# The scan's norm: its sum over partitions behind the next application on TensorE, its reciprocal root as a power on GpSimd

## The reference, cut to what matters

```
y = y + D * x                        # scan's result, 256 tokens x 2048
y = y * silu(z)
y = y * rsqrt(mean(y*y over each group of 256 features) + 1e-5) * norm_w
mix = y @ w_out
x = layer_norm(ALPHA * x + mix, ln1_g, ln1_b)
```

## Time and profile before

| | |
|---|---|
| median of 3 runs | 2312.76 us |
| the profiled execution's own time | 2315.55 us |
| its span | 2313.7 us |
| mean granted TensorE clock | 0.996 |
| TensorE busy | 2276.5 us (98%) |
| VectorE busy | 952.4 us (41%) |
| ScalarE busy | 445.7 us (19%) |
| GpSimd busy | 74.1 us (3%) |

### The profile page before, as it was taken

The page is one execution under the profiler, slowest core; times in us unless marked ns, Lnnn a source line. Parts: engine busy times, 40 slices in busy tenths (PEclk is TensorE's granted clock), DMA queues, the critical chain, the costliest instruction groups (busy, mean ns, idle before and its releaser), DMA issues.

```text
span 2313.7 us, 25295 instructions
## 1 busy us (share of the span) xinstructions
PE 2276.5 (98%) x10678; PEld 1349.9 (58%) x10678; DVE 952.4 (41%) x1905; ACT 445.7 (19%) x1011; POOL 74.1 (3%) x130
## 2 busy tenths in 40 slices
PE   8999999999999999999999999999999999999998
PEld 6568547886487449897434333334999643333343
DVE  3567656667576556553211111123754321211122
ACT  3410003357100010220211211101032021111111
POOL 2000000000100000000000000000000000000000
PEclk9999999999999999999999999999999999999999
DMA  7279625354698414246999999995426599999997
GB/s 291 109 307 398 258 77 204 147 182 182 240 407 319 179 74 179 100 171 266 379 428 427 427 427 428 428 419 194 147 81 246 224 409 427 427 428 427 428 428 289
DMA packets 59167, 671.64 MB, mean 290 GB/s; under 512 B 7504, under 2 KB 7792, under 8 KB 18720
## 3 DMA queue, kind: packets, MB, share of 16 engines
q1 hardware_dynamic: 51888, 649.45, 69.0%
q0 software_dynamic: 7152, 20.43, 2.6%
HBM read 666.59 MB, written 3.26 MB: 290 GB/s over the span
## 4 chain that ended last, share of the span: by engine, by line
PE 88%; DMA 9%; DVE 2%; ACT 0%; issue 0%; SPq 0%; POOL 0%; DVEq 0%; POOLq 0%; ACTq 0%
PE ps L101 85%; DMA ring<-in_exp_w 6%; DMA arena<-in_exp_w 2%; PE ps L349 1%; DVE arena L114 1%; DVE arena L117 1%; PE ps L2698 1%; DMA ring<-in_ada_w 0%; PE ps L625 0%; DMA arena<-ssm_rows 0%; DMA X<-in_x 0%; PE ps L1875 0%; DVE X L117 0%; ACT arena L105 0%; PE ps L1217 0%
## 5 line engine op out<-in xcount | busy, mean ns | idle before, releaser
L101 PE MATMUL ps<-arena 128*64 128x512 f32 (+7 forms) x3956 | 937.5, 467 | 15.2 <-DMA arena<-in_exp_w 5.7
L101 PEld LDWEIGHTS ps<-arena 128*128 128x128 f32 (+2 forms) x3956 | 446.5, 166 | 462.6 <-issue 434.2
L101 PE MATMUL ps<-ring,arena 128*64 128x512 f32 (+1 forms) x1664 | 447.2, 591 | 2.6 <-DMA ring<-in_exp_w 2.6
L101 PE MATMUL ps<-XTGB,ring 128*128 128x256 f32 (+1 forms) x2160 | 423.5, 353 | 0.0
L101 PEld LDWEIGHTS ps<-XTGB,ring 128*128 128x128 f32 x2160 | 367.1, 190 | 52.8 <-issue 10.7
L101 PEld LDWEIGHTS ps<-ring,arena 128*64 128x64 f32 (+1 forms) x1664 | 163.8, 149 | 257.9 <-issue 255.0
L122 DVE COPY arena<-ps 128x512 f32<-128x512 f32 (+3 forms) x135 | 64.9, 500 | 448.5 <-PE ps L101 316.4
L121 ACT COPY arena<-ps 128x512 f32<-128x512 f32 (+3 forms) x181 | 82.7, 477 | 665.8 <-PE ps L101 293.1
L101 PE MATMUL ps<-ring,XTGB 128*128 128x512 f32 (+3 forms) x540 | 208.3, 543 | 0.1
L101 PE MATMUL ps<-XTGB,arena 128*64 128x512 f32 (+2 forms) x736 | 200.7, 428 | 0.0
L105 ACT ACTIVATE arena<-ps 128x512 f32<-128x512 f32 (+2 forms) x95 | 52.2, 555 | 722.4 <-PE ps L101 717.5
(11 more groups left out here) (150 smaller groups left out, 921.5 us busy)
## 6 DMA issues: line engine op xcount, KB each, us to landing
arena<-in_exp_w SPq DMA_DIRECT2D x90, 2048.0 KB, 26.4
ring<-in_exp_w SPq DMA_DIRECT2D x68, 2048.0 KB, 28.1
ring<-in_mlp_w SPq DMA_DIRECT2D x25, 2048.0 KB, 8.7
ring<-in_ada_w SPq DMA_DIRECT2D x20, 2048.0 KB, 9.8
XTGB<-in_exp_w SPq DMA_DIRECT2D x18, 2048.0 KB, 32.1
ring<-in_ssm_w_in SPq DMA_DIRECT2D x12, 2048.0 KB, 7.7
ring<-in_w_in SPq DMA_DIRECT2D x12, 2048.0 KB, 7.8
ring<-in_gate_w SPq DMA_DIRECT2D x12, 2048.0 KB, 7.5
```

What stands on the lines that cost most here:

```text
L101: return self.e.matmul(o, lhsT=lhsT, rhs=rhs, start=start, stop=stop, skip_group_check=True)
```

## The change

1. On TensorE `norm_b(g)` moves from the end of iteration 2g + 4 to iteration 2g + 5, behind the application there (groups 6 and 7 stay where they were). ScalarE's `norm_b` moves likewise, to behind `exps` of the odd iteration.
2. ScalarE does one Identity with scale 1/256 and bias 1e-5 instead of Ln and Exp, and announces `ymean`.
3. GpSimd raises the result to the power -0.5, over 128x256 with `half` broadcast along the row, and announces `yr`. In its program the powers stand among the row loads: power (i - 6)/2 behind load i for even i from 6, and 5 to 7 behind the last load.
4. On VectorE `norm_c` comes one pair of iterations later, for groups 6 and 7 in iterations 18 and 20.

```
+            def norm_power(g):
+                r = xcT[:, 2 * g, :]
+                pool.wait_ge(at("ymean", g), at("half"))
+                pool.then_inc(pool.tt(r, r, C["half"][:, 0:1].to_broadcast([P, T]), ALU.pow), ("yr", g))
...
             for i in range(SP):
                 if i >= 3:
                     pool.wait_ge(at("sy", i - 3))
                 pool.landed(pool.e.dma_start(s_E[i % 3][:, :, 0:512], ...
+                if i >= 6 and i % 2 == 0:
+                    norm_power((i - 6) // 2)
+            for g in range(5, 8):
+                norm_power(g)
...
  (TensorE)
                 if i in (SP, SP + 2):
                     norm_b((i - 4) // 2)
+                elif 5 <= i < SP and i % 2 == 1:
+                    norm_b((i - 5) // 2)
...
-                if 4 <= i < SP and i % 2 == 0:
-                    norm_b((i - 4) // 2)
...
  (ScalarE)
             def norm_b(g):
-                r = xcT[:, 2 * g, :]
                 act.wait_ge(at("sn", g))
-                k = act.then_inc(act.act(r, ps_of("sn", g)[:, 0:T], ACT.Ln, scale=1.0 / 256, bias=epst),
-                                 ("read", "sn", g))
-                act.wait_ge(k)
-                act.then_inc(act.act(r, r, ACT.Exp, scale=-0.5), ("yr", g))
+                act.then_inc(act.act(xcT[:, 2 * g, :], ps_of("sn", g)[:, 0:T], ACT.Identity, scale=1.0 / 256, bias=epst),
+                             ("ymean", g), ("read", "sn", g))
...
                 if i < SP:
                     exps(i)
-                if i >= 4 and i % 2 == 0 and (i - 4) // 2 < 8:
+                if i in (SP, SP + 2):
                     norm_b((i - 4) // 2)
+                elif 5 <= i < SP and i % 2 == 1:
+                    norm_b((i - 5) // 2)
...
  (VectorE)
-                if i >= 5 and i % 2 == 1 and (i - 5) // 2 < 8:
-                    norm_c((i - 5) // 2)
+                if 7 <= i < SP + 2 and i % 2 == 1:
+                    norm_c((i - 7) // 2)
+                if i in (SP + 2, SP + 4):
+                    norm_c((i - 6) // 2)
```

## The result

The changed kernel takes 2605.34 us (median of 4 runs, 2600.05 to 2607.17) against 2313.47 us before (median of 4); the ratio is 1.1251, interval 1.1238 to 1.1264. It is slower by 292 us, where 293 were predicted.

The account below looks back on a forecast made before the run. TensorE was taken to bound the scan, busy 123.33 of 125 us. Eight powers and five gaps on GpSimd delay part (3,0) by 291 us; with 2 us of restart, 2312.8 + 293 = 2606 us, range 2568 to 2642.

Parts of the forecast that it names:

- power 0 starts: GpSimd starts the first power at 513.0 us, after ScalarE's exps(5), Identity of 0.47 us and a handover of 0.1.
- one power: Each of eight 128x256 GpSimd powers takes 41.6 us, from narrower powers' cost of 0.161 us per further element.
- gap, five times: Before powers 1 to 5, GpSimd waits 8.0 us for row load, least, exps, Identity and handovers.
- power 7 ends: GpSimd's last power ends at 886.0 us: 513.0 + 8 x 41.6 + 5 x 8.0 + 0.2.
- delay of (3,0): TensorE's third of the last seven output parts starts at 887.1 instead of 596.15 us, 291 us later.
- restart of TensorE: After idling before part (3,0), TensorE loses 2 us (0 to 5), taken from the program's first eight transposes.
- The removed table loads: On ScalarE, 16 fewer table loads free 20.5 us; worth 0 to 1.7 us to the kernel, taken as 0.
- The sum behind the application: TensorE's sum moved behind the application: with cheap powers, at most 2.4 us lost; in the changed kernel, hidden.
- TensorE idle "some 290 us": TensorE idles some 290 us, nearly all ahead of applications and one output part; its busy time stays as before.
- A cheap power on a long row: On GpSimd, powers below 2.1 us hide before the row loads: no change, 2311 to 2315 us; chance 0.09.
- A price that falls with width: GpSimd's price per element falls somewhat: powers of 10 us give 2353 us, of 20 us 2433; chance 0.05.
- A gain by ScalarE's freed time: ScalarE's freed 24 us bring E earlier, limited to 1.7 us; chance 0.01 of beyond 4.6 us.

Follow-up runs that it names:

- experiment 1: Changed kernel with the eight GpSimd powers acting on only half the columns, 128 of 256; 2440.81 us.
- 5: Changed kernel with the eight GpSimd powers acting on only 32 of the 256 columns; 2323.68 us, ratio 1.0039 to the kernel before.
- 6: Changed kernel with the eight GpSimd powers acting on only 16 of the 256 columns; 2316.46 us, ratio 1.0007 to the kernel before.
- experiment 2: Changed kernel with a multiplication in the power's place on GpSimd, order, waits and queues kept; 2317.43 us, ratio 1.0011 to the kernel before.
- experiment 4: Changed kernel with all 16 row loads issued apart from the powers, on ScalarE's queue instead of GpSimd's; 2566.76 us.
- 9: Changed kernel with 78 idle multiplications of 128x512 on TensorE ahead of output part (3,0); 2604.09 us.
- 10: Changed kernel with 82 idle multiplications of 128x512 on TensorE ahead of output part (3,0); 2606.64 us.
- experiment 8: Changed order with Ln and Exp on ScalarE, moved to the even iteration ahead of the gate's copy, nothing added on GpSimd; 2315.08 us, ratio 1.0005 to the kernel before.
- experiment 3: Changed kernel's order with ScalarE's Ln and Exp instead of Identity, in the odd iteration, nothing added on GpSimd; 2321.46 us, ratio 1.0026 to the kernel before.
- experiment 7: Changed kernel with a multiplication for the power and TensorE's sum back ahead of the odd application; 2316.45 us, ratio 1.0006 to the kernel before.

## Why the prediction was right

| step | predicted | measured |
|---|---|---|
| power 0 starts | 513.0 | 512.32 |
| one power | 41.6 | 41.13 |
| gap, five times | 8.0 | 7.5 to 7.9, sum 38.7 |
| power 7 ends | 886.0 | 879.9 |
| part (3,0) starts | 887.1 | 880.93 |
| delay of (3,0) | 291 | 284.8 |
| restart of TensorE | 2 | 2.5 |

**The price of a power** carried the sum: 333 of the 373 us predicted between power 0's start and power 7's end. The step from 2 and 8 elements to 256 held within 1.1%: 159 ns per element between 8 and 128, and again between 128 and 256. Experiments 1, 5 and 6 show it, and experiment 2 shows that the loss goes with it.

**The gap** was right in its length and in its parts (chain above), and experiment 4 removed it.

**The sum** is 6 us too high in the trace: 3.8 from the powers, 1.3 from the gaps, 0.7 from the start, 0.2 from handovers. Of the 0.7, 0.6 is no error of the working: the first row load left at 474.29 in this execution, at 474.90 in the one of before. That the median still came to within 1 us of 2606 is partly luck: the profiled execution is the fastest of the four, 5.3 us under their median, and behind the scan it took 3 us less than the one of before. Where the others spent more isn't shown.

**The restart** was put at 2 us and took 2.5, but the rows that it was taken from don't bear it. The eight slow transposes of the program's start (1.95 us against 1.04) ran at a granted clock of 1.00 by the profile of before, so their slowness isn't shown to be that of an idle TensorE's clock, and why they were slow stays open. Behind the powers it was the clock, by experiments 9 and 10. This hit is luck in its size.

**The removed table loads** were put at 0. No value shows where ScalarE has slack (the stage took 115.3 us with them in experiment 8, 115.9 and 115.0 without them in 2 and 6). What I hadn't seen is that in the changed order Ln and Exp would have cost some 5 us (experiment 3 against 8); the change removes a cost there that it would itself have brought.

**The sum behind the application** was bounded, with TensorE's idle time, by -1.7 and +2.4 us for cheap powers: 0.3 to 1.2 us in single traces (experiment 7). In the changed kernel it is hidden, as said.

**Three signs were off.** TensorE idle "some 290 us" is 412 - 137 = 275 us in the scan. Of it 24 us lie ahead of the sum of group 7 (799.43), which waits for norm_c(5); the list had only applications and one output part. And its busy time was said to be as before but rose by 12.3 us: the same work at a mean clock of 0.67 takes longer. This costs nothing but at the last restart, the rest lies beside the powers. GpSimd busy 403 us (407 said), row loads 48.8 us apart (49.6), ScalarE's table loads 16 fewer, `least` waiting for loads and TensorE for VectorE: as said.

**The rivals.** A cheap power on a long row: excluded by experiment 1. A price that falls with width: excluded, the widths of 1 to 256 lie on one line. A gain by ScalarE's freed time: no run's median lies below that of before, and 1.7 us of idle TensorE time was all that could have been gained.

## What to carry to other kernels

Price an operation by its own rows at two or more widths and work out the slope; the name of the instruction form (TENSOR_TENSOR of 128x256) says nothing, since here a multiplication took 0.61 us and a power 41.13. Before work is put on a nearly idle queue, list what the queue issues for others: GpSimd was 3% busy, but a row load was due every 6 us, and there was room for 2.9 us of work per pair, but not for 5.4. And a sum over partitions that is the same on all 128 of them makes an engine that pays per row element take every root 128 times over.

## What the runs showed of the hardware

- A power of f32 on GpSimd took 0.556, 0.705, 1.67, 2.92, 5.44, 20.73 and 41.13 us for 1, 2, 8, 16, 32, 128 and 256 elements of the row, all on 128 partitions: about 0.40 us plus 159 ns per element, with steps between neighbouring widths of 149 to 161 ns per element. A multiplication of 256 took 0.61 us.
- TensorE idle for 4.03 us came back at a mean granted clock of 0.91 over the next 17 us, idle for 71.67 us at 0.85, idle for 0.66 us at 1.00. The same five output parts took 18.90, 19.91 and 17.40 us. The cost isn't ordered by length for long idling: behind 33.37 us (half the columns) they took 20.32 us, behind 71.52 us (loads apart) 20.05.
- Some VectorE instructions that began within 0.2 us of the start of a GpSimd one took some 0.3 us longer. In the changed kernel, VectorE's product of 128x512 just behind the start of power 5 (756.55) and the same one in its middle, and norm_c at the start of power 6:

```profile
756.72 0.98 DVE L117 TENSOR_TENSOR arena<-arena 128x512 f32<-128x512 f32 x1
...
768.95 0.69 DVE L117 TENSOR_TENSOR arena<-arena 128x512 f32<-128x512 f32 x1
797.73 1.23 DVE L114 SCALAR_TENSOR_TENSOR arena<-arena 128x256 f32<-128x256 f32 x2 [28.08 <-POOL arena L117]
```

  Before, the product took 0.69 us and norm_c 0.88. In the multiplication run the six such products that began 0.16 us behind a GpSimd multiplication took 0.99 us each, the other two 0.69. The cause was not tested.
